# The first modulation of a two-layer transformer as rows on TensorE, in two halves, with the first products between them

## What is computed

```python
sc = jax.nn.silu(c)                     # (1, 1024)
scc = jax.nn.silu(c_ctx)                # (1024,)
sh1x, sc1x, ... = jnp.split((sc @ w_mod[l] + b_mod[l])[:, None, :], 6, axis=-1)
sh1c, sc1c, ... = jnp.split(scc @ w_mod[l] + b_mod[l], 6, axis=-1)
ux = rmsnorm(h, g_pre_mix[l]) * (1 + sc1x) + sh1x
uc = rmsnorm(hc, g_pre_mix[l]) * (1 + sc1c) + sh1c
...
px = split_cols(ux @ w_in[l])           # the first columns of this are "the first group"
```

## Time and profile before

| what | value |
|---|---|
| median of 3 runs | 1855.46 us (1855.14 to 1858.44) |
| the profiled execution, the run's time | 1860.5 us |
| its span, first to last instruction | 1858.6 us |
| PE busy | 1760.4 us, 95% of the span |
| DVE busy | 1153.9 us, 62% |
| ACT busy | 883.1 us, 48% |
| POOL busy | 584.6 us, 31% |
| DMA, mean over the span | 121 GB/s, in the first fortieth of it 298 GB/s |
| mean granted TensorE clock | 0.981 of full |

### The profile page before, as it was taken

One profiled execution on the slowest core, in us unless ns is written; L12 is line 12 of the kernel. 1 busy time (PEld: TensorE's weight loads), 2 busy tenths in 40 slices (PEclk: granted clock), 3 DMA queues, 4 the chain that ended last, 5 costly groups with the idle time before them and its releaser, 6 DMA issues. The chain is left out here.

```text
span 1858.6 us, 30522 instructions
## 1 busy us (share of the span) xinstructions
PE 1760.4 (95%) x10162; PEld 1491.9 (80%) x10162; DVE 1153.9 (62%) x2344; ACT 883.1 (48%) x1922; POOL 584.6 (31%) x555
## 2 busy tenths in 40 slices
PE   7999999999999999899999999788999999989998
PEld 3777888778788787788888888777898788979997
DVE  4356578677676765567777664456564456756655
ACT  4566555444344443542222223666565455565553
POOL 0354434455455452111111000124335655321100
PEclk8999999999999999999999999999999999999999
DMA  7222233344333235244556663233343323446664
GB/s 298 58 66 66 69 91 92 89 129 120 106 94 95 80 65 168 85 120 148 148 154 207 219 197 69 71 88 87 79 123 104 96 74 86 118 143 180 184 199 159
DMA packets 341254, 224.15 MB, mean 121 GB/s; under 512 B 57654, under 2 KB 322156, under 8 KB 340076
## 3 DMA queue, kind: packets, MB, share of 16 engines
q1 hardware_dynamic: 331692, 215.88, 41.0%
q10 hardware_dynamic: 9408, 6.32, 1.3%
HBM read 221.06 MB, written 1.07 MB: 120 GB/s over the span
## 5 line engine op out<-in xcount | busy, mean ns | idle before, releaser
L1946 PE MATMUL bank<-Uhi,w_ring 128*128 128x512 f32 (+1 forms) x1536 | 547.6, 357 | 18.2 <-ACT H L1628 7.4
L1947 PE MATMUL bank<-Ulo,w_ring 128*128 128x512 f32 (+1 forms) x1536 | 531.5, 346 | 0.0
L1948 PE MATMUL bank<-Uhi,w_ring 128*128 128x512 f32 (+1 forms) x1536 | 531.5, 346 | 0.0
L1488 ACT ACTIVATE w_ring<-load_ring 128x512 fp32r<-128x512 f32 (+3 forms) x632 | 370.0, 607 | 149.0 <-PE bank L1948 104.4
L1693 DVE TENSOR_TENSOR w_ring<-load_ring,w_ring 128x512 fp32r<-128x512 f32 (+1 forms) x424 | 319.6, 770 | 169.3 <-ACT w_ring L1488 150.3
L1946 PEld LDWEIGHTS bank<-Uhi,w_ring 128*128 128x128 f32 x1536 | 294.5, 192 | 59.8 <-ACT H L1628 10.5
L1948 PEld LDWEIGHTS bank<-Uhi,w_ring 128*128 128x128 f32 x1536 | 294.3, 192 | 36.3
L1443 POOL TENSOR_TENSOR w_ring<-load_ring,w_ring 128x512 fp32r<-128x512 f32 (+3 forms) x208 | 246.2, 1189 | 245.4 <-ACT w_ring L1488 140.7
L1947 PEld LDWEIGHTS bank<-Ulo,w_ring 128*128 128x128 f32 x1536 | 295.0, 192 | 29.8
L1431 POOL TENSOR_TENSOR Y<-Y,small 128x512 f32<-128x512 f32 x160 | 173.1, 1082 | 292.5 <-DVE small L1892 279.6
L1897 DVE TENSOR_TENSOR Z<-bank,Z 128x512 fp32r<-128x512 f32 x160 | 109.7, 686 | 96.2 <-ACT Z L1614 95.4
(11 more groups left out here) (142 smaller groups left out, 2661.8 us busy)
## 6 DMA issues: line engine op xcount, KB each, us to landing
load_ring<-in_w_in SPq DMA_DIRECT2D x192, 256.0 KB, 2.9
load_ring<-in_w_ffn_in SPq DMA_DIRECT2D x160, 256.0 KB, 3.1
mod_ring<-in_w_mod SPq DMA_DIRECT2D x96, 256.0 KB, 3.2
load_ring<-in_w_ffn_out SPq DMA_DIRECT2D x88, 256.0 KB, 3.4
mod_place<-in_w_mod SPq DMA_DIRECT2D x64, 256.0 KB, 2.8
load_ring<-in_w_branch SPq DMA_DIRECT2D x64, 256.0 KB, 2.9
mod_w<-in_w_mod SPq DMA_DIRECT2D x8, 1024.0 KB, 15.9
load_ring<-in_w_in SPq DMA_DIRECT2D x64, 128.0 KB, 2.5
```

The costliest lines, as they stand in the source:

```text
L1488: act.activation(w_ring[:, plan.slot['w', key], 0, 0:sz], load_ring[:, plan.slot['load', key], 0:sz], ACT.Copy).then_inc(sem['w_hi'], 1)
L1946: pe.matmul(dst, lhs[0], rhs[0], start=start, stop=False)
L1947: pe.matmul(dst, lhs[0], rhs[1], start=False, stop=False)
L1948: return pe.matmul(dst, lhs[1], rhs[0], start=False, stop=stop)
```

## The change

The first modulation is done on PE alone, all 16 x 128 columns as rows, in two halves. Half 0 has columns 0 to 511 of the shift and of the scale, which is what operand tiles 0 to 3 need; half 1 has the others, for tiles 4 to 7. Each half of each weight tile has a load of its own (0.5 MB, rows of 2 KB) and a semaphore of its own. DVE's sums and PE's column sums are gone, as are `mod0_acc` and `mod0sum`.

The list is rearranged: half 0's products, turn, `mod0add` and `coef0` come before the group, half 1's tiles 0 and 1 too; its tiles 2 to 4 and 5 to 7 are placed behind the first two tiles of the group, its turn behind the third, and the operand step of tile 4 behind that.

Besides: x is loaded first, and the squares of x wait for x alone, those of the context for the context. Two of the four normalising steps move to DVE (`un0d`), and the copies of the odd x tiles too (`xevd`). The parameter transposes move ahead of the x transposes. The two conditioning vectors, the first constants and the 24 small loads of biases and gains are issued by ACT and not by SP, ahead of all of ACT's other work. Only two weight splits, not four, come before the first turn.

The diff, its core:

```diff
-MOD0_DVE = 7 * P
-MOD0_ROWS = ((5, MOD0_DVE, 512), (6, MOD0_DVE + 512, 512), (7, MOD0_DVE + 1024, 128))
+MOD0_BANKS = ((5, 6), (3, 7))
...
     for tt in range(NTOK // P):
         p.step('xsq', tt)
-    for kt in (1, 2):
-        p.step('mod0', kt)
     p.step('mstat', nm, nh=1, dim=D, n=NTOK, after=('x_squares', NTOK // P - 1))
     for tt in range(NTOK // P):
-        p.step('un0', tt)
...
+        p.step('un0d' if tt % 2 else 'un0', tt)
+    first_rows(0, range(5))
     for l in range(DEPTH):
         p.take('acc', ('par', l), ('par_done', l))
         p.step('par', l)
-    p.step('mod0turn', 0)
...
+    turn_in(range(2))
+    first_rows(0, range(5, 6))
+    turn_in(range(2, 4))
+    first_rows(0, range(6, KT))
+    p.step('mod0row', 0)
+    turn_in(range(4, 6))
+    first_columns(0)
+    turn_in(range(6, KT))
+    first_rows(1, range(2))
...
-                if kt < KT:
+                if kt < KT and kt != 4:
                     normed((nm, 0, kt), 0, 0, None, NTOK)
                 if kt:
                     p.step('apB', (nm, 0, kt - 1), side=None, cols=NTOK)
+                    first_rows(1, ((), (), (2, 3, 4), (5, 6, 7), (), (), (), (), ())[kt])
+                    if kt == 3:
+                        p.step('mod0row', 1)
+                    if kt == 4:
+                        first_columns(1)
+                        normed((nm, 0, kt), 0, 0, None, NTOK)
                     p.step('gmm', (first, kt - 1), side=0, both=False)
...
+            for i in range(2):
+                sp.dma_start(H[:, 2 * i:2 * i + 2, :], x_rows[i]).then_inc(s_x[i], 16)
+            first_mod(0)
+            for at, (what, key) in enumerate(plan.loads):
+                if at == L_RING:
+                    first_mod(1)
...
+                    for part, b in enumerate(MOD0_BANKS[h]):
+                        ins = pe.matmul(bank[b][0:2, :], sc[:, :, kt], mod0_w[:, h, kt, part, :], start=kt == 0,
+                                        stop=kt == KT - 1)
```

More of the change, by code:

```diff
@@ L355, in build_plan, with turn_in, first_rows, first_columns @@
     nm = (0, 'pre_mix')
-    p.step('mod0', 0)
+    def turn_in(tiles):
+        for kt in tiles:
+            even = kt % 2 == 0
+            p.take('acc', ('xin', kt), ('xin_left' if even else 'xin_right', kt))
+            p.step('xin', kt)
+            p.step('xev' if even else 'xevd', kt)
+    def first_rows(h, kts):
+        for kt in kts:
+            p.step('mod0', (h, kt))
+    def first_columns(h):
+        p.step('mod0turn', h)
+        p.step('mod0add', h)
+        p.step('coef0', h)
     for tt in range(NTOK // P):
         p.step('xsq', tt)
-    for kt in (1, 2):
-        p.step('mod0', kt)
     p.step('mstat', nm, nh=1, dim=D, n=NTOK, after=('x_squares', NTOK // P - 1))
     for tt in range(NTOK // P):
-        p.step('un0', tt)
[L364 to L372, removed]
+        p.step('un0d' if tt % 2 else 'un0', tt)
+    first_rows(0, range(5))
     for l in range(DEPTH):
@@ L998, in build_plan @@
         piece = st[0] in ('mm', 'mm_a', 'gmm', 'gmm_a', 'gmm_b', 'ym', 'ym_a', 'ym_b')
[L999 removed]
+        if piece or st[:2] == ('mod0turn', 0):
             first = len(begun) if st[1] not in begun else len(begun) - 1
[L1001 removed]
+            while done < min(len(use), first + (AHEAD if piece else 2)) and (
                     done <= first or done < W_RING or use[done - W_RING] in used):
@@ L1063, in build @@
         mod_load = [es.enter_context(nc.semaphore(f"mod_load{k}")) for k in range(RINGS['mod1'])]
-        mod0_load = [es.enter_context(nc.semaphore(f"mod0_load{k}")) for k in range(KT)]
+        mod0_load = [[es.enter_context(nc.semaphore(f"mod0_load{h}{k}")) for k in range(KT)] for h in range(2)]
         s_first = es.enter_context(nc.semaphore("s_first"))
@@ L1068, in build @@
         s_rows = es.enter_context(nc.semaphore("s_rows"))
-        s_x = es.enter_context(nc.semaphore("s_x"))
+        s_x = [es.enter_context(nc.semaphore(f"s_x{i}")) for i in range(2)]
         s_init = es.enter_context(nc.semaphore("s_init"))
@@ L1326, in _ @@
-            for k in range(1, KT):
-                sp.dma_start(mod0_w[:, k, :], w_mod[0, k * P:(k + 1) * P, 0:MOD0]).then_inc(mod0_load[k], 16)
-            for what, key in plan.loads:
-                if what == 'consts':
[L1330 to L1341, removed]
@@ new lines, in first_mod @@
+            def first_mod(h):
+                for k in range(KT):
+                    sp.dma_start(mod0_w[:, h, k], w_mod[0, k * P:(k + 1) * P, 0:MOD0].rearrange("p (a h m) -> p a h m", a=2, h=2)[:, :, h])\
+                        .then_inc(mod0_load[h][k], 16)
+            for i in range(2):
[4 more added lines that the diff above has]
+                    first_mod(1)
+                if what == 'consts':
@@ L1465, in _ @@
         def _(act):
+            act.dma_start(crows[0:8, 0, :], c.rearrange("b (k p) -> (b k) p", p=P)).then_inc(s_c, 16)
+            act.dma_start(crows[8:16, 0, :], c_ctx.rearrange("(k p) -> k p", p=P)).then_inc(s_c, 16)
+            act.dma_start(C[:, 0:NFIRST], consts[:, 0:NFIRST]).then_inc(s_first, 16)
+            for l in range(DEPTH):
+                act.dma_start(rows[0:48, l, :], b_mod[l].rearrange("(k p) -> k p", p=P)).then_inc(s_rows, 16)
+                for i, g in enumerate((g_pre_mix, g_post_mix, g_pre_ffn, g_post_ffn)):
+                    act.dma_start(rows[48 + 8 * i:56 + 8 * i, l, :],
+                                 g[l].rearrange("(k p) -> k p", p=P)).then_inc(s_rows, 16)
+                act.dma_start(rows[80:82, l, :], g_a_q[l].rearrange("(k p) -> k p", p=P)).then_inc(s_rows, 16)
+                act.dma_start(rows[82:83, l, :], g_a_kv[l:l + 1, :]).then_inc(s_rows, 16)
+                for i, g in enumerate((g_d_q, g_d_k)):
+                    for half in range(2):
+                        act.dma_start(rows[83 + i:84 + i, l, half * DH:(half + 1) * DH],
+                                     g[l:l + 1, :]).then_inc(s_rows, 16)
+                act.dma_start(sink[:, l, :], sink_b[l:l + 1, :].to_broadcast([P, 8])).then_inc(s_rows, 16)
             for kind, key, f in steps:
```

122 lines of the change are left out of this document (58 added, 64 removed).

## The result

| | before | after |
|---|---|---|
| median of 7 runs each, on one chip | 1855.46 us (1854.65 to 1858.44) | 1860.72 us (1858.70 to 1862.91) |
| ratio after to before | | 1.0024 (1.0015 to 1.0034) |
| profiled execution: time, span | 1860.5, 1858.6 us | 1860.04, 1857.1 us |
| mean granted TensorE clock in it | 0.981 | 0.989 |
| the first group's last product ends | 67.88 us | 71.74 + 1.09 = 72.83 us |

The forecast was +3.9 us. The runs give +5.3 us, 0.28% by the medians, 0.24% by the ratio. The two profiles alone would say nothing: their times differ by 0.5 us. The execution profiled of the kernel before was 5 us above its own median. So what is compared here is the head of the program (up to the end of the first group), and the rest by the runs.

A forecast was written before the change was run, and what follows sets the result against it. TensorE, busy 95% of the span, was taken as the bound. Later first group end +3.1 us plus clock 0.8 gave +3.9 us on 1855.46, so 1859.4 us; range 1855.5 to 1869.

The forecast's parts named there:

- The unit of 0.86 us for a product: First modulation on TensorE: a product is two 512-column instructions, 0.86 us; 32 products take 27.5 us at full clock.
- 58.5 us of work from start to group end: TensorE from first new product to group end: 56.2 us of work plus 2.3 us lost to half clock at first.
- The start at 12.5 us: TensorE's first product follows ScalarE's load issues (to 9.9 us), table load (to 11.2) and 1.23 us from sigmoid to copied vector.
- Group end 71.0 us: First group's last product: 12.5 + 58.5 = 71.0 us against 67.88, a cost of +3.1 us.
- 0.8 us for a fall of the clock at 31 to 34 us: TensorE's transposes and two-column turns without a wide product may drop the clock: 0.8 us taken, ends nothing and 1.7.
- The cover: Weight tiles, normalised x (cover 3.9 us) and coefficients arrive before TensorE wants them; the second turn costs 0 to 0.5, taken 0.
- That the changed kernel starts from the profile's 67.88 us: The one profile's first group end, 67.88 us, was the base against which the new 71.0 us was set.
- That what lies around the span stays: Outside the span no term was given; +3.9 us was added to the run of 1860.5 us with span 1858.6.
- B, the stall: SP's full queue also stops ScalarE's load issues, adding 8.2 us to the start: +12.1 us, 1867.6; chance 0.18.
- C, the landing sets the start: Tile 0's landing at 9.8 us, not ScalarE, sets TensorE's start: +1.2 us, 1856.7; chance 0.12.
- D, small transfers don't overlap: Each 0.52 MB weight tile stands alone at 3.5 us, so the group ends at 91 us: +23 us, 1878; chance 0.02.
- E, the kernel gets faster: Kernel faster by over 3.7 us, needing the group to end before 64.2 us; chance 0.06.

The follow-up runs named there:

- 2: The kernel before, with conditioning vectors, first constants and the 24 row loads issued by ScalarE ahead of its other work: 1857.40 us, ratio 1.0009.
- run 4: run 1 with the scale columns of half 1 summed on DVE and 16 column sums on TensorE in place of 8 products: 1856.94 us, ratio 1.0015.
- 6: run 5 with the scale columns of half 1 summed on DVE as in run 4: 1861.53 us, ratio 1.0033 to the kernel before.
- 8: The kernel before, unaltered, measured and profiled again: 1857.03 us, ratio 1.0006.
- 9: The kernel before, unaltered, for a third profile: one run of 1857.06 us.
- 7: The changed kernel, unaltered, measured again: 1861.56 us, ratio 1.0032 to the kernel before.
- run 1: The changed kernel with the 24 row loads issued by ScalarE behind the sigmoid, not ahead of it: 1860.14 us, ratio 1.0028 to the kernel before.
- run 5: run 1 with `c`, first constants on SP and two half 0 tiles ahead of x, half 0's products ahead of x transposes: 1860.99 us, ratio 1.0021.
- 10: run 5 with four tiles of half 0, not two, loaded ahead of x: 1860.82 us, ratio 1.0026 to the kernel before.
- Run 3: The changed kernel without interleaving, all products of both halves and both turns ahead of the group: 1868.85 us, ratio 1.0076 to the kernel before.

## Why the prediction was right, and which terms were off

The side, the mechanism and the order of the terms held: the hole goes, the start hardly moves, and the sums that DVE did beside the transfers now lie on TensorE. The size was short by 1.4 us, and partly right by luck: the group end came 1.8 to 2.2 us later than the 71.0 us of the work and the start, the time around the span grew by 0.7 us that no term had, and against that the 0.8 us for the clock did not come, and less half clock behind the head gave something back. Point by point:

- *The unit of 0.86 us for a product.* 12 instructions took 46.96 - 41.72 = 5.24 us, 0.87 for two. Held.
- *58.5 us of work from start to group end.* 59.14. The 32 products with the low clock of the start took 30.6 us (24.95 - 13.69 = 11.26, and the others 19.3), where the forecast had 27.5 + 2.3. The transposes of x took 4.15, as forecast. The turns were cheaper, 34.19 - 33.61 = 0.58 us for eight, 1.2 and not 2.0; so were the parameter transposes, 0.2 and not 0.45. The group was dearer: a tile with products between took 41.72 - 38.74 = 2.98 us and not 2.76, 23.0 in all and not 22.1 (0.16 of it is the end of the last product, 72.83 - 69.91 = 2.92). What makes the 0.2 was not tried.
- *The start at 12.5 us.* 13.69. The mis-sized term is the issues: 10.24 us for 27, not 9.15. The forecast had carried SP's durations over. On ScalarE the first took 0.60 us, b_mod 0.67 and 0.51, most others 0.27 to 0.40. The table load was 1.28 us, as taken; from its end to the first product 1.40 and not 1.23 us.
- *Group end 71.0 us.* 72.83 and 73.23.
- *0.8 us for a fall of the clock at 31 to 34 us.* None came. The granted clock of the stretch behind the start:

```profile
18.90:72.83 53.93, 53.93 (x205) 26.11 (x202) 15.49 (x29) 24.53 (x45) 8.22 (x7) 1.00 0.52 173
```

Against the earlier trace rows, the stretch at half clock from 37.7 to 48.0 us is gone. The one at the start is still there, as the spacing shows: 11.26 us for 20 instructions, 8.7 at full clock, so 2.5 us lost for the 2.3 forecast. Of the two rows on which the forecast could not decide, transposes and column sums, the runs speak for the sums: all six profiles of kernels that have column sums ahead of or in the group (before, 2, 4, 6, 8, 9) fall to half clock within the sums or at most 1.4 us behind them, and none of those without (changed, 7, 1, 5, 10) falls between 22.6 us and the group's end, for all their transposes and two-column turns. Run 3 does, behind its hole. No run alters the sums alone. So the term had no cause here, and the absence of the stretch is a gain of the design that the forecast counted as a loss.
- *The cover.* Every claim held. TensorE waited for no tile after its start, and the tile that it would have waited for landed at 10.06 us (run 1; forecast 9.8). The normalised x was there at 18.72 + 2.19 = 20.9 us (forecast 20) and wanted at 25.15. Tile 4 of the group followed the second turn and tile 3 without idle time.
- *That the changed kernel starts from the profile's 67.88 us.* One profile was taken as the kernel's own. Its usual group end is 67.0 us, and the change is worth +6.0 there, not +4.95.
- *That what lies around the span stays.* It rose from 1.9 to 2.6 us, in every kernel with the two halves and in none of the others. These are medians: 9 of the 58 executions of these kernels stayed under 2.1 us. That is 0.7 us which the forecast had no term for; its cause was not found.

The rivals. B, the stall: ScalarE issued a load every 0.38 us while SP's own queue was held up, eight issues in 7.99 us:

```profile
1.73 7.99 SPq L1339 DMA_DIRECT2D mod_w<-in_w_mod  x8
9.76 4.93 SPq L1387 DMA_DIRECT2D load_ring<-in_w_in  x4
```

So a full queue of SP doesn't stop ScalarE's issues here, and the blocking that the prediction inferred from the Trainium skill, page "DMA: Bandwidth & Descriptors", section "Why a DMA increments its semaphore by 16 and not by 1", did not show in the issues. That the loads themselves landed late is another matter (run 1). C, the landing sets the start, is false for the changed kernel. Run 1 made it true, and the group ended 2.5 us earlier, near C's 2.7, though x was then late by 1.3 us; the median didn't follow (1860.1). D, small transfers don't overlap, is false: in the changed kernel the tiles of 0.52 MB arrive as fast as TensorE takes them, though at 380 to 400 GB/s and not 421. E, the kernel gets faster, is false: the group ended at 72.8 us and not before 64.2.

The range held. The chance for slower, 0.54, was on the right side, by little: the prediction had set the bound at 3.7 us, and the interval of the first result reaches from 2.8 to 6.3 us.

## What to carry to other kernels

Ask of a reduction on an idle vector engine what covers it before moving it to TensorE: here it lay beside the transfers, and TensorE's own part took some 15.5 us of products and 3.3 to 4.15 us of column sums; all of it on TensorE took 28 us at full clock, while the hole that the move removed was 2.4 us wide. When small loads change their queue, look at what the new issuer has to do next; 24 issues of a third of a microsecond each stood ahead of the one short operation on which everything waited. And before costing a sum against one profile, see whether that execution is a usual one: its time against the median, and its stretches at half clock.

## What the runs showed of the hardware that was not expected

- **A small load can land late while another queue moves large ones.** In run 1, two loads of 4 KB issued by ScalarE at 0.74 and 1.38 us landed at 6.0 us, with 2 MB of x issued by SP from 0.74 us on, and the constants behind them at 7.9 us. Issued at the head of SP's own queue, they were used at 2.5 us (run 5) and 2.69 us.
- **TensorE's first products were slow whatever the clock column says.** In run 5 at 5.8 to 12.2 us (columns as above) the granted clock reads 1.00, but eight instructions stand 0.80 us apart, where later ones stand 0.44. The clock's records begin only at 11.4 us there, and before them the column shows 1.00. The spacing of equal instructions is the better witness.

```profile
5.80:12.20 6.40, 6.36 (x8) 0.85 (x8) 0.00 (x0) 0.73 (x1) 0.00 (x0) 1.00 0.94 357
```

- **A hole is followed by half clock, often.** With the waits of 3 to 4 us in the head of runs 3, 5 and 10 went stretches of 3.4 to 6.9 us at half clock, mostly in the products behind them. The first tile of the group in run 3 took 5.3 us for 2.8. So such a hole cost some 1.4 to 2.5 us beyond its own width, which no wait shows.
- **Column sums without a hole were followed by it too.** In run 4 the 16 sums end at 53.4 us and the half clock runs from 54.6 to 58.0 us; in the kernel before it begins at 37.7 us, within the 28 sums. It is not a rule: the 16 sums at 73.6 us of that profile have full clock behind them.
- **Two-column turns cost 0.07 us each** at full clock, where the earlier trace rows had given 0.12 at half clock.
